# Sparse-attention heads of a streaming encoder step: the loop over head pairs written out, reciprocals transposed by TensorE, values multiplied four query tiles at a time

## What is computed

```
logits = jnp.einsum('bthd,btkhd->bthk', q, k_sel) * (HEAD_DIM ** -0.5)
logits = jnp.where(valid[:, :, None, :], logits, -jnp.inf)
probs = jax.nn.softmax(logits, axis=-1)
out = jnp.einsum('bthk,btkhd->bthd', probs, v_sel)
```

## Time and profile before

| | |
|---|---|
| median of three runs | 1770.56 us |
| the profiled execution's own time | 1767.36 us |
| its span (first to last instruction) | 1765.7 us |
| granted TensorE clock, mean over the span | 0.975 of full |
| attention block in the span | 453.5 to 665.7 us |
| TensorE, VectorE, ScalarE, GpSimd busy, share of the span | 92%, 53%, 37%, 28% |

### The profile page before, as it was taken

How to read it: one execution, slowest core, us unless ns; L and a number is a source line. 1 busy time by engine, 2 the same in 40 slices (tenths; PEclk the granted TensorE clock), 3 DMA queues, 4 the chain that set the end, 5 groups by cost and what they waited for, 6 DMA issues and landing times. The chain is left out here.

```text
span 1765.7 us, 23638 instructions
## 1 busy us (share of the span) xinstructions
PE 1623.6 (92%) x8451; PEld 1395.7 (79%) x8451; DVE 939.1 (53%) x1501; ACT 644.6 (37%) x1322; POOL 487.8 (28%) x335
## 2 busy tenths in 40 slices
PE   5988999999687788999899999999999999999995
PEld 5975999877455556879777989888888889888884
DVE  6338999895665565530855333343443333434438
ACT  6346577943566564322633211111111111111112
POOL 5133112147633423212113322121212221121116
PEclk9999999999789999999999999999999999999999
DMA  5122211111100004313233211111011111111006
GB/s 196 57 66 64 82 47 38 58 63 40 31 28 27 2 25 147 126 50 106 84 120 105 63 49 36 48 36 48 26 46 48 48 48 36 48 36 48 25 23 179
DMA packets 88189, 108.16 MB, mean 61 GB/s; under 512 B 6080, under 2 KB 65216, under 8 KB 88128
## 3 DMA queue, kind: packets, MB, share of 16 engines
q1 hardware_dynamic: 88128, 107.35, 20.0%
HBM read 88.05 MB, written 19.28 MB: 61 GB/s over the span
## 5 line engine op out<-in xcount | busy, mean ns | idle before, releaser
L155 POOL TENSOR_TENSOR w_lo_ring<-w_raw_ring,w_hi_ring 128x1024 fp32r<-128x1024 f32 (+1 forms) x97 | 237.6, 2461 | 815.4 <-ACT w_hi_ring L149 814.9
L1959 DVE TENSOR_TENSOR f_y<-f_y,ps 128x512 f32<-128x512 f32 (+1 forms) x288 | 195.7, 685 | 257.6 <-PE ps L200 257.6
L186 PE MATMUL ps<-hth,w_hi_ring 128*128 128x384 f32 (+2 forms) x1176 | 267.8, 331 | 4.2 <-PEq L1643 1.8
L186 PE MATMUL ps<-htl,w_hi_ring 128*128 128x384 f32 (+2 forms) x1176 | 266.3, 330 | 0.0
L186 PE MATMUL ps<-hth,w_lo_ring 128*128 128x384 f32 (+2 forms) x1176 | 266.3, 330 | 0.0
L200 PE MATMUL ps<-w_hi_ring,f_fh 128*128 128x512 f32 (+1 forms) x576 | 226.8, 394 | 18.8 <-DVE f_y L1959 18.8
L200 PE MATMUL ps<-w_hi_ring,f_fl 128*128 128x512 f32 (+1 forms) x576 | 224.7, 390 | 0.0
L200 PE MATMUL ps<-w_lo_ring,f_fh 128*128 128x512 f32 (+1 forms) x576 | 224.6, 390 | 0.0
L186 PEld LDWEIGHTS ps<-hth,w_hi_ring 128*128 128x128 f32 (+1 forms) x1176 | 203.6, 189 | 8.2 <-issue 5.4
L186 PEld LDWEIGHTS ps<-hth,w_lo_ring 128*128 128x128 f32 (+1 forms) x1176 | 202.8, 188 | 0.6
L186 PEld LDWEIGHTS ps<-htl,w_hi_ring 128*128 128x128 f32 (+1 forms) x1176 | 202.8, 188 | 0.6
(11 more groups left out here) (240 smaller groups left out, 2640.2 us busy)
## 6 DMA issues: line engine op xcount, KB each, us to landing
w_raw_ring<-in_w SPq DMA_DIRECT2D x64, 512.0 KB, 3.8
w_raw_ring<-in_w_in SPq DMA_DIRECT2D x24, 512.0 KB, 3.8
n_xin<-in_x_prompt SPq DMA_DIRECT2D x8, 512.0 KB, 5.8
w_raw_ring<-in_w_o SPq DMA_DIRECT2D x8, 512.0 KB, 4.0
oe_x<-in_x_prompt SPq DMA_DIRECT2D x8, 512.0 KB, 4.3
x<-oe_new SPq DMA_DIRECT2D x8, 512.0 KB, 5.0
me_x<-x SPq DMA_DIRECT2D x8, 512.0 KB, 4.1
x<-me_new SPq DMA_DIRECT2D x8, 512.0 KB, 5.0
```

Source lines behind the costliest of these rows:

```text
L155: pool.tensor_tensor(self.lo[:, slot, 0:width], self.raw[:, g % 2, 0:width], self.hi[:, slot, 0:width].bitcast(F32), ALU.subtract).then_in ...
L186: last = pe.matmul(c.ps[0:width, bank + b, 0:size], part[:, slot, k * width:(k + 1) * width], x[:, k, o:o + size], start=(k == 0 and n == ...
L1959: dve.tensor_tensor(out, out, ps[0:r, u % 2, :], ALU.add).then_inc(y_added, 1)
```

## The change

All of it is in `attend_heads`.

- The loops over pairs are written out: 72 units `g` in one row on each engine, with waits on constants.
- The tiles of a head come in the order 0, 7, 1, 6, 2, 5, 3, 4, 8. `x` is a unit's place in this order.
- The pass over mask and maximum is given the factor -1/8 and a minimum, so that it leaves the negated logits and their least value; L1276 goes, and the exponential takes scale -1.
- L1282 and L1285 go: rows are no longer scaled ahead of the transposes. Reciprocals are taken for four tiles in one instruction (new L1326). TensorE transposes each column of reciprocals, spread over 128 columns (new L1392), so that every partition has the factors along its row; ScalarE copies these to `h_rsum` (new L1255, L1259); VectorE multiplies them into the outputs as these leave PSUM (new L1337, L1341), in place of ScalarE's L1203 and L1205.
- The product with the values comes three times in a head, behind x = 6 (tiles 0 to 3, bank 6), x = 7 (tiles 4 to 7, bank 7) and x = 8 (sample, bank 6). Of four tiles, the first two go to partitions 0 to 63 and the last two to 64 to 127, each 256 columns, one instruction for either half in turn.
- For tiles 4 to 7 VectorE copies the first group of transposed blocks (new L1315), ScalarE the others.
- The values have two buffers.

```
+            for g in range(UNITS + 5):
+                if g < UNITS:
...
+                    dve.tensor_tensor_reduce(out=s.rearrange("p (b n) -> p b n", b=n), in0=ps[0:r, 2 * (g % 2):2 * (g % 2) + n, 0:LIM[i] // n],
+                                             in1=c.mask[0:r, MOFF[i]:MOFF[i] + LIM[i]].rearrange("p (b n) -> p b n", b=n),
+                                             scale=-(HD ** -0.5), scalar=-LEAST, op0=ALU.add, op1=ALU.min, accum_out=low[0:r, g % 3:g % 3 + 1]).then_inc(masked, 1)
+                if 0 <= g - 2 < UNITS:
+                    copies(g - 2)
+                if 0 <= g - 3 < UNITS and (g - 3) % NT in LEAVE:
+                    reciprocals(g - 3)
+                if g >= 5 and (g - 5) % NT in LEAVE:
+                    leave(g - 5)
```

The end of the product, and the order on TensorE:

```
+                    for j in range(4 * q + 4):
+                        for a in range(2):
+                            i0 = 4 * q + 2 * a
+                            if j > i0 + 1:
+                                continue
+                            half = slice(64 * a, 64 * a + 64)
+                            if j <= i0:
+                                at = MOFF[i0] // P + j
+                                moving = tiles[:, at:at + i0 + 2:i0 + 1, :]
+                                out = ps[half, 6 + q, 0:256].rearrange("p (t n) -> p t n", t=2)
+                            else:
+                                moving = tiles[:, MOFF[i0 + 1] // P + j, :]
+                                out = ps[half, 6 + q, P:256]
+                            last = pe.matmul(out, v[:, j, :], moving, start=(j == 0), stop=(j == i0 + 1))
+                last.then_inc(pv_done, 1)
+
+            for g in range(UNITS + 4):
+                if g < UNITS:
+                    logits(g)
+                if 0 <= g - 2 < UNITS:
+                    transposes(g - 2)
+                if 0 <= g - 3 < UNITS and (g - 3) % NT in EVENT:
+                    output(g - 3)
+                if g >= 4 and (g - 4) % NT in LEAVE:
+                    sums(g - 4)
```

More of the change, by code:

```diff
@@ L1134, in attend_heads @@
+    assert m.at <= stacks.at
     m.at = stacks.end
     sm = m.put("h_s", [P, 3, SEQ])
[L1136 to L1144, removed]
@@ L1159, in sample_out, with pieces_before, pieces_end @@
-    def sample_out(hh):
-        return ps[0:HD, 2 * ((hh * NT + NP) % 2) + 1, 0:DEC]
+    low = m.put("h_low", [P, 4])
+    ORDER = [0, 7, 1, 6, 2, 5, 3, 4, NP]
+    UNITS = HEADS * NT
+    EVENT = {6: 0, 7: 1, 8: NP // 4}
+    EVENTS = list(EVENT)
+    LEAVE = {6: 0, 7: 1, 8: 2}
+    PIECES = 5
+    assert all(max(ORDER.index(i) for i in range(4 * q, 4 * q + 4)) == x for x, q in EVENT.items() if q < NP // 4)
+    def pieces_before(hd, part):
+        return PIECES * hd + 2 * part
+    def pieces_end(hd, part):
+        return PIECES * hd + min(2 * part + 2, PIECES)
@@ new lines, in unit, with blocks_of, on_dve @@
+    def unit(g):
+        return g // NT, g // NT // 2, g // NT % 2, ORDER[g % NT]
+    def blocks_of(i):
+        return [list(range(a, min(a + 4, i + 1))) for a in range(0, i + 1, 4)] if i < NP else [[0, 1, 2]]
+    def on_dve(i, n):
+        return NP // 2 <= i < NP and n == 0
+    groups = []
+    for g in range(UNITS + 2):
+        if g < UNITS:
+            groups += [(g, n) for n in range(len(blocks_of(unit(g)[3])))]
+        if g >= 2 and (g - 2) % NT in LEAVE:
+            groups.append((g - 2, "sums"))
@@ L1180, in _, with copies @@
         @block.scalar
         def _(act):
[L1182 to L1188, removed]
+            def copies(g):
+                hd, p, hh, i = unit(g)
+                if pv_before(g) > 0:
+                    act.wait_ge(pv_done, pv_before(g))
+                for n, blocks in enumerate(blocks_of(i)):
+                    if on_dve(i, n):
+                        continue
+                    q = first_group[g] + n
@@ new lines, in copies @@
+            def copies(g):
+                hd, p, hh, i = unit(g)
+                for n, blocks in enumerate(blocks_of(i)):
+                    if not on_dve(i, n):
+                        continue
+                    q = first_group[g] + n
+                    if pv_before(g) > 0:
+                        dve.wait_ge(pv_done, pv_before(g))
+                    dve.wait_ge(tr_done, q + 1)
+                    dve.tensor_copy(pt[:, MOFF[i] + blocks[0] * P:MOFF[i] + (blocks[-1] + 1) * P], ps[:, 4 + q % 2, 0:len(blocks) * P]).then_inc(dve_copied, 1)
@@ L1287, in _, with logits @@
         @block.tensor
         def _(pe):
-            def transposes(p, u):
-                hh, i = u // NT, u % NT
+            def logits(g):
+                hd, p, hh, i = unit(g)
                 r = rows_of(i)
-                scaled.wait(pe, p, u + 1)
-                for n, blocks in enumerate(groups[i]):
-                    q = turn(u) + n
-                    tr_out.wait(pe, p, q - 1)
-                    if i == NP:
-                        pe.sem_inc(gate, 1)
+                if g % NT == 0:
+                    stack_hi.wait(pe, p, 3 * hh + 3)
+                    stack_lo.wait(pe, p, 3 * hh + 3)
+                if g >= 2:
+                    pe.wait_ge(masked, g - 1)
+                k0 = 0 if i < NP else SEQ
+                for b, n in enumerate(halves(LIM[i])):
+                    for q, keys in enumerate((kh, kl)):
+                        last = pe.matmul(ps[0:r, 2 * (g % 2) + b, 0:n], qs[:, hh, tok(i)], keys[:, hh, k0 + b * n:k0 + b * n + n],
+                                         start=(q == 0), stop=(q == 1))
+                last.then_inc(qk_done, 1)
```

273 lines of the change are left out of this document (149 added, 124 removed).

## The result

The changed kernel took **1750.04 us** (median of 4 runs, 1744.89 to 1751.01), the kernel before 1770.82 beside it: a ratio of 0.9879, interval 0.9857 to 0.99. The forecast was 1743, with the range from 1724 to 1768. The profiled execution took 1749.91 us, its span is 1747.8. Timed once more beside three experiments, the change took 1748.5 us, ratio 0.9872 (0.9847 to 0.9896).

A forecast was written before the change was run, and what follows sets the result against it. No engine fills the attention block; handing work round bounds it. Block: 20.5 + seven heads 151.9 + 12.8 = 185.2 us, 27 under 212.2; 1767.4 - 27 = 1740.4, plus 3.2 for the median, hence 1743 us, range 1724 to 1768.

The forecast's parts named there:

- The open price, side by side: Product with the values: the array's halves overlap, so tiles 0 to 3 take 1.5 us, tiles 4 to 7 3.25.
- rival (a): Product with the values: halves run one after another, or other waits cover the gain; 3 us less, median 1767; chance 0.22.
- Rival (b): Product with the values: each change of half drains the array, 2.5 us a head; slower, median 1787; chance 0.08.
- (c): Rival: TensorE's clock stays at 1.2 GHz over the attention block, which takes 260 us; median near 1818; chance 0.04.
- the low clock shows once: Sign that the forecast is right: in the attention block the low clock comes only at the block's start.
- stretch 1: First part of a head, from the end of tile 4's exponential: TensorE works without a pause, 7.9 us (10.9 without overlap).
- stretch 2: Second part of a head: handing round of reciprocals, multiplication, sample's product, logits, mask and exponential between engines, 7.3 us.
- stretch 3: Last part of a head: ScalarE's exponentials of tiles 2, 5, 3, 4, copies and waits, 6.5 us.
- Head splits on ScalarE stay, at x = 1, 2, 3 of every second head, where ScalarE waits for TensorE anyway: ScalarE's splits (1.322 us) are covered by its waits; without that cover they would cost 3.75 us a pair.
- the filling until the first tile 4: Start of the attention block, 20.5 us: ScalarE's work 13.3, filling and waits 4, low clock 3.
- The four drains go: The stalls at the ends of the pairs of heads disappear, but for the last; no size of its own.
- No scaling next to GpSimd's splits: VectorE's scalings, dear beside GpSimd's splits (768 columns 1.329 us, 1024 columns 0.755), are gone; also named as a sign.

The follow-up runs named there:

- Experiment 1: The changed kernel with each product with the values done for one half of the array, then the other, not in turn: 1763.86 us.
- experiment 10: The changed kernel with tiles in order 0 to 7, sample, ScalarE's head splits earlier, and the halves one after another: 1738.57 us.
- experiment 2: The changed kernel with ScalarE's three head splits of a pair moved earlier, so that GpSimd starts sooner: 1739.65 us.
- experiments 3 and 5: 3: the changed kernel with the sample's product one slot later, 1737.75 us; 5: the same with ScalarE's head splits also earlier, 1720.5 us.
- experiment 6: The changed kernel with a head's query tiles in the plain order 0 to 7, then sample: 1721.96 us.
- experiment 4: The kernel before with only the loops over pairs of heads written out, on all five engines: 1768.9 us.
- Experiments 7 and 8: 7: the changed kernel with VectorE scalings by one put back ahead of the transposes, 1791.7 us; 8: those scalings after the transposes, 1762.62 us.

## Why the prediction held, and where it did not

**The open price, side by side: right.** The walk took the lower bounds, 1.5 and 3.25 us; 1.66 and 3.39 came. Experiment 1 turns the gain off and gives back 14 us, which ends rival (a)'s first half (halves one after another). Its second half (covered by other waits) falls for the heads without GpSimd's stop, where all of the 1.78 us show, and for the plain order, where experiment 10 has most of them in every head; in the change's heads with the stop, a shorter stop and the clock made up for it. The sentence cited from the Trainium skill, "TensorEngine Tiling (Array Packing)", section Key Properties, agrees with the trace, with a condition that the page doesn't name: 5.17 us where the halves follow each other, 3.39 where they alternate. The rule of the same page of the Trainium skill, section PSUM Bottleneck, by which (a) would have come, didn't decide here: 14 us were gained with the emptying of PSUM as it was. Rival (b), a drain at each change of half, is out: the run of 14 would take 8 us.

**The clock: half right.** (c) is out, as the window from the first exponential of tile 4 to the last one shows (second row, clock 0.95):

```profile
453.40:468.10 14.70, 10.54 (x55) 7.96 (x56) 8.31 (x21) 13.48 (x26) 5.94 (x2) 0.88 0.44 129
468.10:629.20 161.10, 126.56 (x843) 93.53 (x842) 76.92 (x212) 98.17 (x242) 78.78 (x37) 0.95 0.07 19
```

But "the low clock shows once" failed: it shows in the middle of the pairs too (0.56 and 0.66 in the first two). The ground given for it, that the clock fell where a pair started and stayed up elsewhere, didn't hold in the kernel before either, where it also fell inside the first pair:

```profile
485.20:488.90 3.70, 3.35 (x13) 1.92 (x12) 3.63 (x6) 1.30 (x4) 3.53 (x2) 0.64 0.00 0
```

**The head: 21.7 us walked, 20.9 measured when nothing hinders it.** From the end of one exponential of tile 4 to the next (494.4 to 515.2), stretch 1 took 8.5 us (walked 7.9), stretch 2 6.9 (7.3), stretch 3 5.4 (6.5). VectorE's idle stretch between heads is 3.2 us where nothing hinders, just over the 3 that was named as a sign, and up to 4.4 around GpSimd's stops. Prices of new operations were close. VectorE's copy took 688 ns (697 taken), its product of 64x256 421 (424), ScalarE's copy 379 (383), as these groups of the changed kernel show:

```profile
L1315 DVE COPY h_pt<-ps 128x512 f32<-128x512 f32 x32 | 22.0, 688 | 4.9 <-PE ps L1404 4.9
L1341 DVE TENSOR_TENSOR cat<-ps,h_rsum 64x256 f32<-64x256 f32 x32 | 13.5, 421 | 10.4 <-ACT h_rsum L1259 8.8
...
L1259 ACT ACTIVATE h_rsum<-ps 64x256 f32<-64x256 f32 x32 | 12.1, 379 | 25.7 <-PE ps L1392 24.9
```

**The step that failed** is "Head splits on ScalarE stay, at x = 1, 2, 3 of every second head, where ScalarE waits for TensorE anyway". For ScalarE itself the cover held: in experiment 2 heads with the splits and without them take 20.9 us alike. But the cover was judged for ScalarE alone, and the splits did not stay. Behind them GpSimd makes the low parts, and TensorE waits for those. In the new order they come later after a pair's first logits, GpSimd is done after 22.7 us instead of 18.5, and the 2.7 us of slack are gone. Four heads took 24.6 us on average instead of 20.9 ((161.0 - 3 x 20.86) / 4, with 161.0 us from the first exponential of tile 4 to the last). Experiment 2 shows it. That these 3.7 us a pair are near the 3.75 that the forecast named for a lost cover is chance: that price was ScalarE's own time, and this one is GpSimd's lateness and the lower clock behind it.

**The sum** came within 7 us by luck: its errors met. The seven heads took 161.0 us, 9.1 over the 151.9 forecast; the filling until the first tile 4 took 14.7 (the first row above) instead of 20.5 (the terms named add to 20.3), 5.8 under: ScalarE's 13.3 were right (13.48), but of the 7 us for waits and the low clock only 1.2 came. The last rest took 13.1 (12.8). Block: 3.6 over. With the 5.5 us lost behind it, 1767.4 - 23.4 + 5.5 = 1749.5, near the 1749.91 of the profiled execution; the 3.2 us that the forecast added for the median are not there any more (1750.04 against 1749.91).

**Two terms that were not in the sum as terms.** Stretch 2 has the sample's product wait ("Only then may TensorE do the sample's product"): it was walked as part of the way, rightly, and experiments 3 and 5 show that it needn't be there. And the order of the tiles was taken as given, with no price; experiment 6 gives it one, 28 us against the change. "The four drains go" was named without a sum of its own, and by the rows it is where the gain lies. In the kernel before, 21.2 us pass from the first logits of a pair to those of its second head, and 32.6 from there to the next pair (507.26, 528.46, 561.02); now it is 22.8 and 22.2 (494.51, 517.32, 539.50). Writing out the loops brings 2 us of this (experiment 4). Which of the other edits takes the drain away was not tried in the kernel before, and neither VectorE's share of the copies nor the second buffer of the values was tried alone.

**"No scaling next to GpSimd's splits"** was in the forecast as a reason. Experiments 7 and 8 show what it is worth in this kernel: 42 us, two thirds of it by the chain.

## What to carry to other kernels

When a change shortens or reorders a stage, list for every engine that feeds it, also two engines back, how long before its need its work is done; the shortest slack is the next wait (here GpSimd's 2.7 us, behind copies on ScalarE that were themselves hidden). Two halves of the PE array gave their full gain here only where the program alternates between them. Price an order of units as one edit of its own: here the plain order, or ScalarE's splits and one product moved, was worth more than the change (1720.5 against 1750.0 us, from 1770.8).

## What the hardware did that was not expected

- Two products on the two halves of the array overlap only near each other in TensorE's order: alternating, 14 take as long as the longer half (3.39 us); one half after the other, 5.17, about 0.45 us under the serial sum of 5.6 (estimated from 0.216 us for a record of the kernel before).
- A VectorE scaling from SBUF to SBUF doesn't slow down beside GpSimd's subtraction, it stands until that ends: 2.99 us for 256 columns. All 20 scalings of experiment 7 that began during one of GpSimd's subtractions ended 0.1 to 0.6 us behind its end. VectorE's mask with one input from PSUM isn't touched (0.94 to 0.96 us in either case). The Trainium skill says this on the page "SBUF — State Buffer", section "Who interferes with whom": a shared pair of ports, held by one of the two for a whole instruction. The trace agrees (ends at 518.08 and 517.93).
- In the change's first profile all four stops of TensorE in the middle of a pair, 1.7 to 2.5 us, came with the lower clock level for the product behind them (3.1 us instead of 1.66 in the second pair), and the waits of 1.6 us before the sample's product, from head to head, did not. That is no rule: in its second profile a stop of 0.8 us came without the lower level, and in experiment 1 the clock was low behind the sample's product in five heads (0.50 at 484.8 to 488.2 us).
